# Ends of layers in a two-block transformer: embedding product, shared norms, earlier rounding of panels

## What is computed

```python
x = x + merged @ w_out[l]
x = x + jnp.square(jax.nn.relu(rmsnorm(x, norm_ffn_g[l]) @ w_ff1[l])) @ w_ff2[l]
h = rmsnorm(x, final_norm_g)                       # between the blocks
for i in range(DEPTH_2):                           # 2
    u = rms_norm(h, attn_norm_w[i])
    ...                                            # forgetting attention, retention
    h = h + mixed @ w_out[i]                       # mixed: 8 heads of each, ret is group-normed
    h = h + gated_conv_ffn(rms_norm(h, ffn_norm_w[i]), w_up[i], conv_w[i], conv_b[i], w_down[i])
    gate = jax.nn.sigmoid(rms_norm(h, ple_norm_w[i]) @ w_ple_gate[i])
    h = h + gate * (p[i] @ w_ple_proj[i])          # p: 512 x 256
return rms_norm(h, final_norm_w)
```

## Time and profile before

| | us |
|---|---|
| median of three runs | 2589.0 |
| profiled execution | 2587.95 |
| its span | 2585.9 |
| TensorE busy | 2416.5 |
| GpSimd, VectorE, ScalarE busy | 1169.4, 1114.6, 893.0 |

### The profile page before, as it was taken

How to read it: one execution, slowest core, us unless ns; L and a number is a source line. 1 busy time by engine, 2 the same in 40 slices (tenths; PEclk the granted TensorE clock), 3 DMA queues, 4 the chain that set the end, 5 groups by cost and what they waited for, 6 DMA issues and landing times.

```text
span 2585.9 us, 37430 instructions
## 1 busy us (share of the span) xinstructions
PE 2416.5 (93%) x11548; PEld 1902.0 (74%) x11548; DVE 1114.6 (43%) x1861; ACT 893.0 (35%) x1364; POOL 1169.4 (45%) x1570
## 2 busy tenths in 40 slices
PE   7999895999999999799989999997999889999996
PEld 5776673677788888577667888886777667888874
DVE  2466566443322223435554434342345544343443
ACT  3354342444322222324324322243323234322253
POOL 5334541225455455433225656555533135645553
PEclk9999997999999999899999999999999999999998
DMA  4221111114232222222113323222211112323222
GB/s 142 82 84 48 45 53 33 49 58 129 90 107 96 89 97 96 70 82 65 65 41 103 104 89 102 89 90 83 90 58 65 65 56 99 106 90 104 86 86 81
DMA packets 62813, 211.21 MB, mean 82 GB/s; under 512 B 7008, under 2 KB 7392, under 8 KB 62736
## 3 DMA queue, kind: packets, MB, share of 16 engines
q1 hardware_dynamic: 56160, 194.27, 22.8%
q10 hardware_dynamic: 6576, 15.97, 1.9%
HBM read 208.05 MB, written 2.16 MB: 81 GB/s over the span
## 4 chain that ended last, share of the span: by engine, by line
issue 48%; POOL 35%; PE 14%; DVE 1%; POOLq 1%; DVEq 1%; ACT 0%; ACTq 0%
POOL w_lo L1595 35%; PE acc L256 4%; PE acc L257 3%; PE acc L258 3%; PE po L485 1%; PE sc L485 1%; PE sc L385 0%; PE po L333 0%; PE pt L317 0%; DVE cums L1182 0%; POOLq L1624 0%; POOLq L1601 0%; POOLq L1592 0%; DVE probs L1029 0%; DVEq L1189 0%
## 5 line engine op out<-in xcount | busy, mean ns | idle before, releaser
L1595 POOL TENSOR_TENSOR w_lo<-raw,w_hi 128x256 fp32r<-128x256 f32 x1506 | 1128.6, 782 | 1335.2 <-ACT w_hi L638 1332.5
L256 PE MATMUL acc<-act_hi,w_hi 128*128 128x512 f32 x2000 | 821.0, 411 | 48.1 <-DVE act_lo L1026 36.3
L257 PE MATMUL acc<-act_lo,w_hi 128*128 128x512 f32 x2000 | 789.7, 395 | 0.0
L258 PE MATMUL acc<-act_hi,w_lo 128*128 128x512 f32 x2000 | 789.6, 395 | 0.0
L638 ACT CAST w_hi<-raw 128x1024 fp32r<-128x1024 f32 (+1 forms) x390 | 394.0, 1020 | 360.1 <-PE acc L258 189.9
L256 PEld LDWEIGHTS acc<-act_hi,w_hi 128*128 128x128 f32 x2000 | 381.8, 191 | 158.2 <-issue 42.6
L258 PEld LDWEIGHTS acc<-act_hi,w_lo 128*128 128x128 f32 x2000 | 381.4, 191 | 82.6
L257 PEld LDWEIGHTS acc<-act_lo,w_hi 128*128 128x128 f32 x2000 | 382.9, 191 | 71.1 <-issue 2.2
L256 PE MATMUL acc<-y_hi,w_hi 128*128 128x512 f32 x880 | 353.9, 402 | 27.7 <-DVE y_lo L1046 12.1
L257 PE MATMUL acc<-y_lo,w_hi 128*128 128x512 f32 x880 | 347.3, 395 | 0.0
L258 PE MATMUL acc<-y_hi,w_lo 128*128 128x512 f32 x880 | 347.2, 395 | 0.0
(11 more groups left out here) (275 smaller groups left out, 2186.7 us busy)
## 6 DMA issues: line engine op xcount, KB each, us to landing
raw<-in_w_ffn_wide SPq DMA_DIRECT2D x120, 512.0 KB, 3.3
raw<-in_w_in SPq DMA_DIRECT2D x104, 512.0 KB, 3.3
raw<-in_w_rest SPq DMA_DIRECT2D x72, 512.0 KB, 3.3
raw<-in_w_gate SPq DMA_DIRECT2D x24, 512.0 KB, 3.3
raw<-in_w_ple_gate SPq DMA_DIRECT2D x16, 512.0 KB, 3.2
raw<-in_w_branch SPq DMA_DIRECT2D x24, 256.0 KB, 2.6
raw<-in_w_ffn_narrow SPq DMA_DIRECT2D x16, 384.0 KB, 3.0
x<-in_x ACTq DMA_DIRECT2D x16, 256.0 KB, 3.1
```

What stands on the lines that cost most here:

```text
L256: nc.tensor.matmul(dst, w[0], src[0], start=start, stop=False)
L257: nc.tensor.matmul(dst, w[0], src[1], start=False, stop=False)
L258: return nc.tensor.matmul(dst, w[1], src[0], start=False, stop=stop)
L1595: last = nc.gpsimd.tensor_tensor(w_lo[:, slot, cut], raw[:, slot % 2, cut], w_hi[:, slot, cut], ALU.subtract)
```

## The change

- Every norm: TensorE runs **two** panels up to their seventh k-tile, then both last k-tiles, then the sum matmuls (`first_two`); ScalarE rounds panels 2 and 3 before it makes the factor (`two_more`), and what follows skips those two (`skip`). This holds for the start, the norm of block 1's network, the block change and both layers' norms.
- Block change: the squares of x and of x times `mid_g` are summed in one pass over the tiles, while the last chunk is added to x; the tiles for the next gemm are x times `mid_g` times the attention gain (`mid_attn`, made once near the start on VectorE). `mid_factor` derives both factors. The second square of a tile runs on ScalarE, the second sum on VectorE. The wait for the second set of constants moves behind the 13 panels that follow.
- Retention tail: panels 2 and 3 of the projection are rounded before the squares; their first four k-tiles, and those of panels 0 and 1, run between the group norm's sums (`fox_half`).
- Layer tails: the embedding split moves beside the FFN's first chunk; the embedding product comes before the gate panels and is copied to SBUF by ScalarE; the gates are taken tile by tile, product, addition to x and next norm's tile each in turn. Layer 1's inputs lie in `y_hi`, `y_lo` from tile 4. The last norm's gain is applied by ScalarE in the tail, the factor by five products on VectorE and three on GpSimd.
- The loops over the two layers are written out on SyncE, TensorE, ScalarE and VectorE, and the first FFN tile pair and the first hidden chunk on ScalarE too.
- The embedding panels are loaded before the gate panels (`SEGMENTS2`); the sizes stay.

The core of the diff (eight columns of indent are cut; left out: the sum of both squares, the hidden chunks' loops, argument lists, the moved embedding split):

```diff
-O_GATE, O_PLE = 105, 113
+O_PLE, O_GATE = 105, 108
...
             pe.wait_ge(S("const_loaded"), 32)
         pe.wait_ge(S("norm_total"), r + 1)
-        nc.tensor.matmul(sc[:, 0, :], c["ones"], probs[:, 0, :], start=True, stop=True).then_inc(S("norm_sum"), 1)
-    def normed_gemm(layer, first, count, r, split):
-        gemm(layer, first, 1, KD, act_in, (S("norm_split"), split * 8))
+        last = nc.tensor.matmul(sc[:, 0, :], c["ones"], probs[:, 0, :], start=True, stop=True)
+        if r == 2:
+            last = nc.tensor.matmul(sc[:, 1, :], c["ones"], probs[:, 1, :], start=True, stop=True)
+        last.then_inc(S("norm_sum"), 1)
+    def first_two(layer, first, r, src, base):
+        for j in range(2):
+            pe.wait_ge(lo_done, layer + (first + j + 3))
+            pe.wait_ge(acc_free, layer + (first + j + 1))
+            tile_products(acc[:, (first + j) % 4, :], (first + j) % 4, 0, P, KD, src, base,
+                          None if j else (S("norm_split"), r * 8), range(KD - 1))
+        pe.wait_ge(S("norm_split"), r * 8 + KD)
+        for j in range(2):
+            tile_products(acc[:, (first + j) % 4, :], (first + j) % 4, 0, P, KD, src, base, None,
+                          range(KD - 1, KD)).then_inc(gemm_done, 1)
+    def normed_gemm(layer, first, count, r, src=act_in, base=0):
+        first_two(layer, first, r, src, base)
         norm(r)
-        gemm(layer, first + 1, count - 1, KD, act_in)
+        gemm(layer, first + 2, count - 2, KD, src, base=base)
...
+        def fox_half(j):
+            slot = (O_O + j) % 4
+            pe.wait_ge(lo_done, layer + (N_BLOCK1 + O_O + j + 3))
+            pe.wait_ge(acc_free, layer + (N_BLOCK1 + O_O + j + 1))
+            tile_products(acc[:, slot, :], slot, 0, P, KD, y_in, part=range(4))
         for p in range(PAIRS):
-            head_mean("r_o", l * 4 + (p + 1), "r_mean", p, wa[:, p, :])
+            head_mean("r_o", l * 4 + (p + 1), "r_mean", p, wa[:, p, :], ret_bank)
+        fox_half(0)
         for p in range(PAIRS):
-            head_mean("r_sq", l * 4 + (p + 1), "r_var", p, wb[:, p, :])
-        gemm(layer, N_BLOCK1 + O_O, 8, KD, y_in, (S("r_y"), l * 4, 4))
+            head_mean("r_sq", l * 4 + (p + 1), "r_var", p, wb[:, p, :], ret_bank)
+            if p < 3:
+                fox_half(p + 1)
+        for j in range(4):
+            slot = (O_O + j) % 4
+            for k in range(4, KD):
+                if j == 0:
+                    pe.wait_ge(S("r_y"), l * 4 + (k - 3))
+                last = tile_products(acc[:, slot, :], slot, 0, P, KD, y_in, part=range(k, k + 1))
+            last.then_inc(gemm_done, 1)
+        gemm(layer, N_BLOCK1 + O_O + 4, 4, KD, y_in)
...
-        normed_gemm(layer, N_BLOCK1 + O_GATE, 8, l * 3 + 5, l * 3 + 4)
         pe.wait_ge(S("e_split"), l * 2 + 2)
-        for q in range(3):
+        for m in range(KD):
+            q, bank = m // 3, (O_PLE + m) % 4
             n, slot = layer + (N_BLOCK1 + O_PLE + q), (O_PLE + q) % 4
-            pe.wait_ge(lo_done, n + 3)
-            pe.wait_ge(acc_free, n + 4)
-            for m in range(3 if q < 2 else 2):
-                last = tile_products(acc[:, m, :], slot, m * 2 * P, P, 2, y_in, 8)
-            last.then_inc(gemm_done, 1)
-    norm(9)
+            if m % 3 == 0:
+                pe.wait_ge(lo_done, n + 3)
+            if m < 4:
+                pe.wait_ge(acc_free, layer + (N_BLOCK1 + O_PLE + m + 1))
+            else:
+                pe.wait_ge(S("e_free"), l * 8 + (m - 3))
+            last = tile_products(acc[:, bank, :], slot, (m % 3) * 2 * P, P, 2, y_in, 8)
+            last.then_inc(gemm_done if m in (2, 5, 7) else S("e_done"), 1)
+        pe.wait_ge(S("e_free"), l * 8 + 8)
+        normed_gemm(layer, N_BLOCK1 + O_GATE, 8, l * 3 + 4)
+    norm(8)
...
+    def two_more(half, full, first):
+        for j in range(2):
+            high(half, full, first + LOOK + j)
...
+    def mid_factor():
+        act.wait_ge(S("norm_sum"), 3)
+        factor(mid_rstd, sc[:, 0, :], 1.0 / D, "eps").then_inc(S("mid_rstd"), 1)
+        act.wait_ge(S("mid_square"), 1)
+        factor(rstd[:, :], mid_square, 1.0 / D, "eps").then_inc(S("mid_factor"), 1)
...
-    with act.Fori(0, LAYERS) as l:
+    for l in range(LAYERS):
         half, full = l * (PER_LAYER // 2), l * PER_LAYER
-        ln_exp_table()
-        norm(l * 3 + 3, l * 3 + 2, "attn_w", l * KD)
-        split_ahead(half, full, N_BLOCK1 + O_FL, 3)
+        split_ahead(half, full, N_BLOCK1 + O_FL, 3, skip=2)
...
+        for j in range(2):
+            high(half, full, N_BLOCK1 + O_O + LOOK + j)
         for p in range(PAIRS):
         for p in range(PAIRS):
             act.wait_ge(S("r_var"), l * 4 + (p + 1))
-            factor(wb[:, p, :], mean_bank[p], 1.0, "gn_eps").then_inc(S("r_rstd"), 1)
-        split_ahead(half, full, N_BLOCK1 + O_O, 8,
-                    lambda k, odd: norm_tile(l * 3 + 4, k, odd, l * 3 + 3, "ffn_w", l * KD))
-        norm_factor(l * 3 + 4)
+            factor(wb[:, p, :], ret_bank[p], 1.0, "gn_eps").then_inc(S("r_rstd"), 1)
+        for j in range(KD):
+            if j > 1:
+                high(half, full, N_BLOCK1 + O_O + LOOK + j)
+            norm_tile(l * 3 + 3, j, j % 2, "ffn_w", l * KD)
+        two_more(half, full, N_BLOCK1 + O_FFN[0])
+        norm_factor(l * 3 + 3)
...
+            if ch == 0:
+                two_tiles(0, 2)
+            with act.Fori(1 if ch == 0 else 0, count // 2) as i:
+                two_tiles(i)
...
+            if ch == 0:
+                act.wait_ge(S("e_loaded"), l * 16 + 16)
+                for k in range(2):
+                    nc.scalar.copy(y_hi[:, 8 + k, :], wv[:, k, :]).then_inc(S("e_hi"), 1)
             done += count
+        for m in range(KD):
+            if m % 3 == 0:
+                high(half, full, N_BLOCK1 + O_PLE + LOOK + m // 3)
+            if m in (2, 5, 7):
+                act.wait_ge(gemm_done, full + panel_done(N_BLOCK1 + O_PLE + m // 3))
+            else:
+                act.wait_ge(S("e_done"), l * 5 + (1, 2, 0, 3, 4, 0, 5)[m])
+            settle(act)
+            nc.scalar.copy(wa[:, m, :], acc[:, (O_PLE + m) % 4, :]).then_inc(S("e_free"), 1)
+        act.drain().then_inc(acc_free, 3)
+        two_more(half, full, N_BLOCK1 + O_GATE)
+        norm_factor(l * 3 + 4)
+        for j in range(KD):
+            if j > 1:
+                high(half, full, N_BLOCK1 + O_GATE + LOOK + j)
+            in_place(ACT.Sigmoid, "e_g", "e_gate", l * 8 + j, wb[:, j, :])
+            if j == KD - 1:
+                ln_exp_table()
+            if l + 1 < LAYERS:
+                norm_tile(l * 3 + 5, j, j % 2, "attn_w", l * KD + KD, attn_tiles(l + 1))
+            else:
+                norm_tile(l * 3 + 5, j, j % 2, "final_g", 0, (wb, None, 0))
+        if l + 1 < LAYERS:
+            two_more(half, full, N_BLOCK1 + PER_LAYER)
         norm_factor(l * 3 + 5)
-        act.wait_ge(S("e_loaded"), l * 16 + 16)
-        for k in range(2):
-            nc.scalar.copy(y_hi[:, 8 + k, :], wv[:, k, :]).then_inc(S("e_hi"), 1)
-        split_ahead(half, full, N_BLOCK1 + O_GATE, 8,
-                    lambda j, odd: in_place(ACT.Sigmoid, "e_g", "e_gate", l * 8 + j, wa[:, j, :]))
-        split_ahead(half, full, N_BLOCK1 + O_PLE, 3)
-    ln_exp_table()
-    norm(9)
-    for k in range(KD):
-        act.wait_ge(S("out_ready"), k + 1)
+    for k in (0, 5, 1, 2, 6, 3, 4, 7):
+        act.wait_ge(S("out_ready" if k < 5 else "out_ready_too"), k + 1 if k < 5 else k - 4)
         act.dma_start(out[k * P:(k + 1) * P, :], wb[:, k, :]).then_inc(S("out_stored"), 16)
...
-    dve.wait_ge(S("norm_rstd"), 3)
+    dve.wait_ge(S("mid_rstd"), 1)
+    v.tensor_tensor(mid_square, mid_rstd, mid_rstd, ALU.mult)
+    dve.drain()
+    v.tensor_tensor(mid_square, mid_square, sc[:, 1, :], ALU.mult).then_inc(S("mid_square"), 1)
     for k in range(KD):
-        v.scalar_tensor_tensor(x[:, k, :], x[:, k, :], par("mid_g", k), rstd[:, :], ALU.mult,
-                               ALU.mult).then_inc(S("norm_x"), 1)
-    dve.drain()
-    with dve.Fori(0, LAYERS) as l:
+        v.scalar_tensor_tensor(x[:, k, :], x[:, k, :], par("mid_g", k), mid_rstd, ALU.mult, ALU.mult)
+    dve.wait_ge(S("mid_factor"), 1)
+    v.tensor_tensor(rstd[:, :], rstd[:, :], mid_rstd, ALU.mult)
+    dve.drain().then_inc(S("norm_rstd"), 1)
+    for l in range(LAYERS):
         layer = l * PER_LAYER
-        norm(l * 3 + 3, l * 3 + 2, "attn_w", l * KD)
-        dve.wait_ge(S("norm_rstd"), l * 3 + 4)
+        dve.wait_ge(S("norm_rstd"), l * 3 + 3)
...
-        dve.wait_ge(S("norm_rstd"), l * 3 + 6)
+        dve.wait_ge(S("norm_rstd"), l * 3 + 5)
         settle(dve)
-        evacuate(layer, N_BLOCK1 + O_GATE, 8, lambda i: wa[:, i, :], "e_g")
-        dve.wait_ge(S("e_gate"), l * 8 + 8)
-        for q in range(3):
-            dve.wait_ge(gemm_done, panel_done(layer + (N_BLOCK1 + O_PLE + q)))
-            w = 3 if q < 2 else 2
-            gate = wa[:, 3 * q:3 * q + w, :]
```

(31 more changed lines are left out.)

174 lines of the change are left out of this document (100 added, 74 removed).

## The result

Median 2549.0 us (4 runs, 2547.8 to 2550.3) against 2586.9 for the kernel before on the same chip (4 runs, 2584.9 to 2589.5): ratio 0.9856, 95% interval 0.9844 to 0.9868. The profiled execution took 2547.8. The kernel is faster, as forecast, but by 37.9 us where 19.4 were forecast (2568.5), at the lower edge of the stated range (2549).

The account below looks back on a forecast made before the run. TensorE, busy 93% of the span, was taken as the bound, leaving 169.4 us of idle time, plus half-clock work, to win. Stage gains and losses summed to 19.4 us, giving 2568.5 us from a 2589.0 median; range 2549 to 2584.

Parts of the forecast that it names:

- start, first norm and block change: Program start, first norm of block 1 and change to the next block: gains of 1.0, 5.2 and 8.8 us.
- the wait of 7.3 for panel 5's weights: Block change: ScalarE rounds panel 5 only behind the forget gates' stores, so TensorE waits a new 7.3 us.
- second rival: Gate tiles: ScalarE switches tables between Sigmoid and Square, 31 us in all, giving 2600 us; chance 0.05.
- the wait for y_lo in retention: Retention tail: TensorE waits 2.3 us there, as the last variance's factor and rows come late.
- third rival: Gate tiles: VectorE waits a whole GpSimd operation, 0.74 us, per product and addition: 8 us more, 2576; chance 0.12.
- the second tail: Layer tail 1, to the program's end: 91.7 us where it took 86.4, a loss of 5.3.
- retention tails, FFN norms and layer tails: Stages in both layers: retention tails gain 6.2 us, FFN norms lose 1.2, layer tails gain 4.7 and lose 5.3.
- I charge 1.7 per wait, 2.3 behind a long one.: TensorE's half clock after idle time: 1.7 us lost per wait, 2.3 behind a long one.
- The tile chain: Layer tails: each gate tile is a serial chain, 6.7 us from tile 2 on in tail 0, 6.4 in tail 1.
- convolution to 17.3, table load 1.28: FFN norm: table load and Gelu follow the convolution, ending at 19.3 us, before panel 4's rounding; loss 0.6 each.
- first rival: Layer tails: tile chain hidden, TensorE sets the pace at 5.46 us; 19 us more gain, 2549; chance 0.13.
- The fifth: Rival on the early roundings: they do nothing since transfers land late; five waits of 2.2 us, 2579; chance 0.05.

Follow-up runs that it names:

- the kernel with one panel: Kernel after with one panel ahead of every sum but the program's first, two block-change edits, and all final products on VectorE: 2524.3 us.

## Why the prediction was right and wrong

**Right:** the sign; start, first norm and block change, within 1.2 us each; the wait of 7.3 for panel 5's weights (7.38); no idle ahead of the first norms' sums; gate tiles 6 to 7 us apart in tail 0; no table switch between Sigmoid and Square (second rival); the wait for y_lo in retention (2.3, measured 2.15). The gate tiles' operations beside GpSimd lost 0.59 and 0.38, together 0.97 where the forecast had 0.74 and the third rival 1.48.

**Wrong among its signs:** the second tail was not longer than 86.4 but 0.1 shorter. Two of its sums are off by 0.2 in themselves (91.5 - 82.5 is 9.0, and the terms of tail 1 add up to 91.5), which decides nothing.

**Wrong, in the terms of the sum.** The profiles' 40.4 against 19.4 leaves 21.0: 23.2 more in the retention tails, FFN norms and layer tails, 2.2 less in start, first norm and block change. Three steps make 22.9 of the 23.2:

- *"I charge 1.7 per wait, 2.3 behind a long one."* This is the step that failed most. In the profile of the kernel after, waits of 1.10 to 2.15 us were followed by no half clock: the granted clock is 1.00 over both waits of the retention tail (the second of the four rows of stretches), and over those of the FFN norm and behind the embedding product:

```profile
1356.50:1386.87 30.37, 28.62 (x125) 23.01 (x124) 12.95 (x19) 11.21 (x14) 14.47 (x19) 1.00 0.29 98
1718.70:1750.00 31.30, 30.20 (x132) 24.30 (x131) 4.55 (x7) 14.18 (x20) 16.14 (x23) 1.00 0.29 102
```

  Charged were 1.4 in each retention tail, 1.7 in each FFN norm, 1.7 behind each embedding product, and 2.6 with a short wait in the next layer's panels, where 2.4 was not due: 12.0 in all. The price was read from waits of 2 to 4 us (the earlier trace rows has a matmul of 0.79 behind 2.19), and put on shorter ones. Part of the miss is luck: the same wait of 2.15 in the retention tail, of which there are 26 in the profiles with the halves, was followed by the half clock in 6 of them and by 1.3 us of loss, just what was charged. None of the waits of 1.1 to 1.8 that stand alone was, in any profile. Behind long waits the price of 2.3 was too low once and too high once: the clock of 0.74 over the 10.6 us from 1071.4 is 2.8, and 0.85 over the 9.8 us from 1760.2 is 1.5.
- *The tile chain.* 6.7 a tile from tile 2 on in tail 0 was 6.2 (6.17 to 6.24), and 7.3 and 6.0 ahead of them 6.6 and 5.3: tile 7 came 69.3 us into the tail, not 74.9, 1.7 of which is the clock above. In tail 1 the last sum of squares ended at 73.1, not 79.2, with the same 1.7. Together 8.3. The three gaps of 0.24, 0.42 and 0.27 came from tiles inside loops and were 0.16, 0.14 and 0.04 in the new tiles, 0.59 less; 0.23 more than charged beside GpSimd took part of it back. The prediction knew that the layers are written out, put "0 to 2 us" on it and took the old gaps for the chain all the same. Its own first rival had this mechanism (constant waits cut the gaps), and overstated what follows: from tile 2 on the chain was never as short as a panel in tail 0.
- *"convolution to 17.3, table load 1.28".* The load does not wait for the convolution. ScalarE ran it at once, and Gelu when its data came:

```profile
1369.04 0.63 ACT L718 ACTIVATE rstd<-rstd 128x512 f32<-128x512 f32 x1
...
1369.69 1.28 ACT L1022 ACT_TABLE_LOAD   x1
1373.50 0.63 ACT L1022 ACTIVATE probs_t<-probs_t 128x512 f32<-128x512 f32 x1 [2.53 <-DVE probs_t L1654]
```

  1.3 in each FFN norm, 2.6. With the clock's 1.7 this is more than the whole miss of that term: a loss of 0.6 became a gain of 2.0.

The first rival's 2549 is the measured time to 0.1 us, and not for its reasons: TensorE did not set the pace in tail 0 and did so for two tiles of tail 1, and the tails came out 13.4 above the forecast, not 19. That agreement is luck. The fifth (the early roundings do nothing) is refuted by 38 us.

**What the forecast did not look for** is the other side of a cover. It wrote for the first norm that two panels cover the wait of 3.54, and for the FFN that the factor comes 5.5 later, but never asked whether one panel covers the 3.54 (it does: a panel is 5.46) and what the second then costs. Nor did it say that two panels ahead take away the one behind. Its sum takes the two edits together, and so the forecast had no price for either: 16.5 lost by the one, 38 won by the other.

**Open:** the -2.4 in untouched code of block 1, and 2.4 won in the retention loops and heads. Both lie inside what untouched code differs by between profiles: that stage of block 1 took 463.7 to 469.1 us in the sixteen profiles, the heads and retention loops of a layer 180.9 to 186.3. The retention tail of layer 1 gained 1.0 more than that of layer 0 because it was 1.0 longer before.

## What to carry to other kernels

Cover in front of a reduction is paid for by all that stands behind it: put there as much as the wait is long, and not a panel more (in this kernel 16.5 us), and look at what covers the factor and the next weights on the other side. Price two edits at one place as four corners, since here the one was worth 6 or 38 us depending on the other. Where a chain through two engines takes longer than the pace, look for one engine's part that fits into the other's wait. Moving it one tile behind won 7.9 us in the tails of the kernel with one panel, where earlier weights lost 7.7; in the kernel with two panels the same two edits won 3.6 and 3.4. There the first still has the waits for weights, 6.0 and 5.8, and the second the chain of 6.2 a tile; no run has both.
